# A hybrid block on one Trainium2 core: the second mixer's attention written as one pipeline of 16 heads, and a tile turned ahead of the output products

## The reference

```python
h = rmsnorm_2(x, mix_norm_g)
proj = h @ w_in
qa, ka, va, q_lat, kv_lat, k_r, g_a, g_b = jnp.split(proj, IN_OFFSETS, axis=-1)
qa, ka = apply_rope(qa), apply_rope(ka)               # 8 and 2 heads of 64
o_a = swa_sink_attention(qa, ka, va, sinks)           # 8 heads, window 128
qb = (rmsnorm_2(q_lat, q_norm_g) @ w_uq)              # 384 -> 8 heads of 96
kvb = (rmsnorm_2(kv_lat, kv_norm_g) @ w_ukv)          # 256 -> 8 x (64 key, 64 value)
o_b = mla_attention(q_nope, q_rope, k_nope, k_rope, vb)
y = sigmoid(g_a) * (o_a @ w_o_swa) + sigmoid(g_b) * (o_b @ w_o_mla)
x = x + y @ w_out
x = x + (silu(h @ w_gate) * (h @ w_up)) @ w_down      # h: x, normed again
```

## Time and profile before

| | us |
|---|---|
| median of 3 runs | 1191.82 (1191.3 to 1192.6) |
| the profiled execution | 1191.22 |
| its span in the trace | 1189.4 |
| TensorE matmuls busy | 1135.6 (95%) |
| TensorE weight loads busy | 952.0 (80%) |
| VectorE, ScalarE busy | 693.6 (58%), 587.9 (49%) |
| second mixer, from its norm to the last MLP's norm | 793.6 to 994 |

### The profile page before, as it was taken

How to read it: one execution, slowest core, us unless ns; L and a number is a source line. 1 busy time by engine, 2 the same in 40 slices (tenths; PEclk the granted TensorE clock), 3 DMA queues, 4 the chain that set the end, 5 groups by cost and what they waited for, 6 DMA issues and landing times. The chain is left out here.

```text
span 1189.4 us, 13875 instructions
## 1 busy us (share of the span) xinstructions
PE 1135.6 (95%) x5748; PEld 952.0 (80%) x5748; DVE 693.6 (58%) x777; ACT 587.9 (49%) x830; POOL 23.5 (2%) x35
## 2 busy tenths in 40 slices
PE   5999999999999999999899999999998889999997
PEld 4888887999989877777778888878887777888886
DVE  4644545676677777766575544466755266644443
ACT  4543335454577656654363444266565444444333
POOL 0000000000001100000000000000000000000000
PEclk9999999899999999999999999999998699999999
DMA  9666564555666553355456655545632235656650
GB/s 312 200 194 191 182 191 145 192 178 179 185 199 191 181 187 115 119 166 195 142 177 194 195 178 185 198 137 179 189 131 71 71 116 181 198 178 184 202 180 36
DMA packets 131150, 202.74 MB, mean 170 GB/s; under 512 B 5728, under 2 KB 98784, under 8 KB 130832
## 3 DMA queue, kind: packets, MB, share of 16 engines
q1 hardware_dynamic: 128272, 190.68, 49.9%
q0 software_dynamic: 2816, 11.18, 2.7%
HBM read 200.76 MB, written 1.08 MB: 170 GB/s over the span
## 5 line engine op out<-in xcount | busy, mean ns | idle before, releaser
L898 DVE TENSOR_TENSOR WL<-RAW,WH 128x2048 fp32r<-128x2048 f32 (+1 forms) x181 | 406.0, 2265 | 101.0 <-ACT WH L432 100.8
L432 ACT ACTIVATE WH<-RAW 128x2048 fp32r<-128x2048 f32 (+1 forms) x181 | 338.5, 1890 | 15.1 <-DMA RAW<-in_w_in 6.8
L1440 PE MATMUL PS<-WH,XTH 128*128 128x512 f32 (+1 forms) x700 | 277.7, 397 | 1.9 <-ACT V L622 1.9
L1442 PE MATMUL PS<-WH,XTL 128*128 128x512 f32 (+1 forms) x700 | 273.4, 391 | 0.0
L1441 PE MATMUL PS<-WL,XTH 128*128 128x512 f32 (+1 forms) x700 | 272.7, 390 | 0.0
L1440 PE MATMUL ACC<-WH,KTH 128*128 128x512 f32 (+1 forms) x466 | 186.9, 401 | 9.2 <-DVE KTL L987 6.0
L1441 PE MATMUL ACC<-WL,KTH 128*128 128x512 f32 (+1 forms) x466 | 184.0, 395 | 0.0
L1442 PE MATMUL ACC<-WH,KTL 128*128 128x512 f32 (+1 forms) x466 | 184.0, 395 | 0.0
L1440 PEld LDWEIGHTS PS<-WH,XTH 128*128 128x128 f32 x700 | 131.7, 188 | 28.2 <-ACT V L622 2.3
L1442 PEld LDWEIGHTS PS<-WH,XTL 128*128 128x128 f32 x700 | 131.5, 188 | 27.9
L1441 PEld LDWEIGHTS PS<-WL,XTH 128*128 128x128 f32 x700 | 131.8, 188 | 25.7
(11 more groups left out here) (258 smaller groups left out, 1287.3 us busy)
## 6 DMA issues: line engine op xcount, KB each, us to landing
RAW<-in_w_in SPq DMA_DIRECT2D x48, 1024.0 KB, 5.3
RAW<-in_ffn_w_gate SPq DMA_DIRECT2D x44, 512.0 KB, 4.0
RAW<-in_ffn_w_up SPq DMA_DIRECT2D x44, 512.0 KB, 5.0
RAW<-in_ffn_w_down SPq DMA_DIRECT2D x22, 1024.0 KB, 5.0
RAW<-in_w_gate SPq DMA_DIRECT2D x22, 512.0 KB, 4.1
RAW<-in_w_up SPq DMA_DIRECT2D x22, 512.0 KB, 5.1
RAW<-in_w_down SPq DMA_DIRECT2D x11, 1024.0 KB, 5.0
RAW<-in_ssd_w_branch SPq DMA_DIRECT2D x8, 1024.0 KB, 5.1
```

The source lines that it names most:

```text
L432: nc.scalar.activation(WH[:, s, 0:n], RAW[:, s, 0:n], ACT.Copy).then_inc(w_hi, 1)
L898: tt(WL[:, s, 0:n], RAW[:, s, 0:n], WH[:, s, 0:n].bitcast(F32), ALU.subtract).then_inc(w_lo, 1)
L1440: mm(ps, stat_hi, mov_hi, start=first, stop=False)
L1442: return mm(ps, stat_lo, mov_hi, start=False, stop=last)
```

## The change

**Second mixer, order of the units.** Input chunks are now 512, 512 and 416 columns wide: first the q latent with the window heads' keys, then their queries, then values, kv latent and rope key. The gate chunks `U_G2[0..3]` stand between the other units, the last one between `U_OSWA` and `U_OMLA`.

**Opening.** Each latent is squared, scaled and turned by itself (`latent_squares`, `latent_scale`, `latent_hi`, `latent_lo`); a table load for exp and tanh stands behind the second one. The first latent's squares go to V.

**16 heads in a row.** Round q of 18 does one head: `head_scores(q)` (bank 4), `turn_mla(q - 7)` in rounds 7 to 14, `cover(q)` (12 or 24 weight matmuls: gate pieces, `U_UKV`, `U_OSWA`), `head_values(q - 2)` (bank 6), `head_turn(q - 1)` (bank 5). Window heads are 0 to 7, latent heads 8 to 15. VectorE: `head_max(q)`, `head_sum(q - 1)`, `split_lo` in 11 of the rounds, mostly one after ScalarE's for the same unit, `head_out(q - 2)`. ScalarE: `head_exp(q)`, `split_hi`, gate copies, the copy of head q-1's turned probabilities. Three sets of small results (`head_sm`) and two score tiles take turns.

**Gates.** Copy and sigmoid become one tanh(x/2) as the chunk is copied; the product with a branch is (tanh + 1) times it, and the half is a scale of 0.5 where y is split for `U_OUT2`. y stays in BUF2. `branch_merge` runs in rounds 12 and 13.

**Both output products.** `by_pairs` has `then`: ahead of the last dozen branch matmuls TensorE waits for the first merged quarter and turns it; `second_merge` does product, sum, product, sum and then `kt_lo`; the list of `products` starts with that tile turned (`turned=True`), and its second extra split is at `j == 1`. In the second mixer `mla_piece(1, 1, first_out=True)` does this inside its 12 matmuls.

**First mixer's banks.** Value chunk 0 uses banks 0 and 1, gate chunk 0 banks 4 and 0, with earlier counts to wait for.

Core of the diff:

```diff
@@ banks
-            return ((4, 7), (4, 5), (6, 7), (4, 5))[n][t]
+            return ((4, 0), (4, 5), (6, 7), (4, 5))[n][t]
-            return ((5, 4), (7, 5))[n][t]
+            return ((0, 1), (7, 5))[n][t]
@@ TensorE, first mixer
-                    first_half(u, (v_bank(v, 0), v_bank(v, 1)), lambda t: pe.wait_ge(qkv_kept, ((7, 8), (8, 9))[v][t]))
+                    first_half(u, (v_bank(v, 0), v_bank(v, 1)), lambda t: pe.wait_ge(qkv_kept, 7) if v else pe.wait_ge(conv_done, 12))
-                        first_half(u, (4, 7), lambda t: pe.wait_ge(qkv_kept, 10 + t))
+                        first_half(u, (4, 0), lambda t: pe.wait_ge(qkv_kept, 8 + t))
@@ TensorE, by_pairs
                     if s < 3:
                         turn(s + 1)
+                    elif then:
+                        then()
                     pair_rows(u0 + s // 2 * 2, 1, s % 2, (n0 + s) % 2, False, s >= 2)
...
-            by_pairs(8, U_DAW, XN, turned=True)
-            by_pairs(12, U_WOUT, V, ready=lambda s: pe.wait_ge(merged, (1, 3, 2, 4)[s]))
+            def first_merged():
+                pe.wait_ge(merged, 1)
+                turn_tile(12, V, 0, 0)
+            by_pairs(8, U_DAW, XN, turned=True, then=first_merged)
+            by_pairs(12, U_WOUT, V, ready=lambda s: pe.wait_ge(merged, (1, 3, 2, 4)[s]), turned=True)
@@ VectorE, products and second_merge
-                        if j == n - 1:
+                        if j == 1:
                             split_lo()
...
-                product(0)
-                product(1)
-                own.wait()
-                add(0)
-                add(1)
+                for b in range(2):
+                    product(b)
+                    own.wait()
+                    add(b)
+                kt_lo(20 if m else 12, 0.5 if m else None)
@@ ScalarE, opening of the second mixer
+                if q == 5:
+                    act.wait_ge(proj_kept, 6)
+                    latent_squares(KL0, KV_RANK, 2)
+                    rsqrt(RS[:, 2:4], SS[:, 2:4], 2, lat_rs, 1.0)
+                    nc.scalar.preload_act_table_set("exp_and_others")
...
+            uq_keep(0)
+            split_hi()
             swa_keep(0)
+            uq_keep(1)
             swa_keep(1)
             swa_keep(2)
             split_hi()
+            act.wait_ge(lat_turned, 3)
+            act.wait_ge(w_used, U_UQ + 2)
+            latent_hi("kv_lat", [(7, 0), (7, 1)], (1,))
@@ VectorE, rounds
+            for q in range(18):
+                if q < 16:
+                    head_max(q)
+                if 1 <= q <= 16:
+                    head_sum(q - 1)
+                if q in (1, 2, 3, 5, 7, 9, 11, 12, 13, 15, 16):
+                    split_lo()
+                if q == 0:
+                    query_rope()
...
+                if q >= 2:
+                    head_out(q - 2)
@@ TensorE, before and in the rounds
+            pe.wait_ge(q_kept, 4)
+            g2_piece(0, 0, 0)
             pe.wait_ge(kdup_ok, 1)
+            turn_keys(6)
+            pe.wait_ge(lat_ok, 2)
             pe.wait_ge(swa_kept, 2)
+            turn_latent(7, KL0, 2)
+            pe.wait_ge(proj_kept, 6)
             pe.wait_ge(swa_kept, 3)
+            for q in range(18):
+                if q < 16:
+                    head_scores(q)
...
+                    turn_mla(q - 7)
+                if q < 17:
+                    cover(q)
+                if q >= 2:
+                    head_values(q - 2)
+                if 1 <= q <= 16:
+                    head_turn(q - 1)
```

More of the change, by code:

```diff
@@ L1243, in _ @@
             second_merge(0, BUF1, U_DAW + 3)
-            products(12, U_WOUT, 4)
+            products(12, U_WOUT, 4, turned=True)
             boundary(1, U_WOUT + 3, 4)
@@ L1284, in _, with latent_scale, latent_lo @@
-            dve.wait_ge(swa_roped, 1)
+            def latent_scale(c0, rank, ss, n):
+                dve.wait_ge(lat_rs, n)
+                for t in range(NT):
+                    a = PROJ[:, t, c0:c0 + rank]
+                    ins = ts(a, a, RS[:, ss + t:ss + t + 1], None, ALU.mult)
+                    own.inc(ins) if t == 0 else ins.then_inc(lat_ok, 1)
+            def latent_lo(name, banks, first, last):
+                for j, (bank, k) in enumerate(banks):
+                    dve.wait_ge(lat_hi, first if j < 2 else last)
+                    ins = stt(KTL[:, j * TOK:(j + 1) * TOK], PS[bank][:, k * TOK:(k + 1) * TOK],
+                              COLS[:, GC[name] + j:GC[name] + j + 1], KTH[:, j * TOK:(j + 1) * TOK].bitcast(F32),
+                              ALU.mult, ALU.subtract)
+                ins.then_inc(lat_lo, 1)
@@ new lines, in branch_merge, with head_max @@
+            def branch_merge(t):
+                dve.wait_ge(g2_kept, 4)
+                dve.wait_ge(w_used, U_OSWA + 2) if t else dve.wait_ge(tile_half, HALF[U_OSWA])
+                for h in range(2):
+                    a = BUF2[:, t, h * 512:(h + 1) * 512]
+                    stt(a, a, 1.0, PS[2 * t + h][:], ALU.add, ALU.mult).then_inc(acc_read, 1)
+            nsinks = ROWS[:, ROW["dt_bias"]:ROW["dt_bias"] + 8]
+            def head_max(q):
+                dve.wait_ge(sc2, q + 1)
+                if q >= 2:
+                    dve.wait_ge(p2_turned, q - 1)
+                mx, nmax, sums, sink, rec = head_sm(q)
+                r = q % SWA_HEADS
+                own.link(tt(SC[q % 2], PS[4][:, 0:384], tab("swa" if q < SWA_HEADS else "mla"), ALU.add))
+                for i in range(NT):
+                    own.inc(nc.vector.tensor_reduce(mx[:, i:i + 1], SC[q % 2][:, i * P:i * P + P * (i + 1)], AX.X, ALU.max))
+                own.wait()
+                if q < SWA_HEADS:
+                    ts(nmax, mx, -HD ** -0.5, nsinks[:, r:r + 1], ALU.mult, ALU.min).then_inc(s2_ready, 1)
+                else:
+                    ts(nmax, mx, -MLA_QK ** -0.5, None, ALU.mult).then_inc(s2_ready, 1)
@@ L1555, in pair_rows, with by_pairs @@
                     ins.then_inc(tile_half, 1)
-            def by_pairs(n0, u0, src, ready=None, turned=False):
+            def by_pairs(n0, u0, src, ready=None, turned=False, then=None):
                 def turn(s):
@@ L1773, in _ @@
[L1773 to L1780 removed]
+            pe.wait_ge(proj_kept, 4)
+            up_queries(1)
+            turn_queries(1, 7)
@@ L1855, in _ @@
+            cover(17)
+            pe.wait_ge(o2_kept, 16)
+            turn_rows(19, XN, 6)
+            mla_piece(0, 1)
+            pe.wait_ge(k_lo, 20)
+            mla_piece(1, 0)
+            mla_piece(1, 1, first_out=True)
+            by_pairs(20, U_OUT2, BUF2, ready=lambda s: pe.wait_ge(merged, 4 + (1, 3, 2, 4)[s]), turned=True)
             norm(4, U_FFN3)
```

615 lines of the change are left out of this document (320 added, 295 removed).

## The result

| | before | changed |
|---|---|---|
| median | 1191.56 us (4 runs) | 1169.09 us (1168.5 to 1170.6, 4 runs) |
| ratio | | 0.982, 95% interval 0.981 to 0.984 |
| the profiled execution | 1191.22 | 1170.61 |
| its span | 1189.4 | 1168.8 |

Faster by 22.5 us in the medians and by 20.6 in the two profiled executions. The forecast was 18.6 less, 1172.6, with a range of 1164 to 1184.

A forecast was written before the change was run, and what follows sets the result against it. TensorE, busy 95% of the span, was taken as the bound, with only its idle and low-clock time to win. Terms -1.6 - 2.8 - 2.1 - 7.7 - 3.1 - 1.3 = -18.6 gave 1172.6 us, range 1164 to 1184.

The forecast's parts named there:

- A: First mixer's gate chunk 0: the 1.92 us wait before it goes, between 0 and 1.9 won, taken as -1.6 us.
- B: First output product: its second weight unit starts earlier, though TensorE idles some 2 us for a split; -2.8 us.
- F: Second output product: same form as the first, TensorE idles 1.6 us, too short for the clock to fall; -3.1 us.
- C: Norm behind the first output product: an earlier split removes 1.7 of the 2.57 us gap and 0.4 of slow matmuls; -2.1 us.
- G: Norm behind the second mixer: the add moves 2.2 us forward and the 1.30 us gap closes; -1.3 us.
- E: Second mixer up to its branch's end: -11.1 us, less 3.4 for two dips of the clock, gives -7.7 us.
- E, the opening: Second mixer's start: TensorE waits 2.5 us for ScalarE's query copies and 3.2 before scores 1, each followed by low clock.
- E, the rounds: Second mixer's head rounds and what follows to the branch's end: 108.2 us, with covers narrowly hiding VectorE and ScalarE.
- q7 to q9 5.2 each: Second mixer's rounds 7 to 9: priced at 5.2 us each, 15.6 together.
- Rival 2: VectorE or ScalarE sets the second mixer's round: 0.85 us more in each of 16 rounds, 1186 us; chance 0.09.
- Rival 3: Clock stays at 1.2 GHz in the second mixer's chopped rounds, making the kernel slower: 1212 us; chance 0.04.
- rival 1: Smoother second-mixer opening: ScalarE's row overlaps better or the clock doesn't fall, 1166 us; chance 0.15.

The follow-up runs named there:

- Experiment 7: Changed kernel with the gate pieces of heads 13 and 14 moved to round 15, leaving two rounds without a cover: 1174.9 us.
- Experiment 5: Changed kernel with the second weight unit's low part computed earlier on VectorE in both output products: 1164.4 us.
- experiment 6: Changed kernel with the last split of both output products moved behind the norm's first residual sum: 1168.5 us.
- Experiment 2: Changed kernel with the doubled split of both output products back in their last step, as before: 1173.1 us.
- experiment 3: Changed kernel with ScalarE's table load moved from behind the kv latent's scale to just ahead of the copy of the turned keys: 1168.4 us.
- experiment 4: Changed kernel with two opening splits moved: ScalarE's behind the kv latent's high part, VectorE's behind head 0: 1164.9 us.
- experiment 8: Changed kernel with VectorE's mask sum of every head done three times, 1.1 us more a round for 16 rounds: 1174.9 us.

## Why the prediction was right, and where not

- **What bounds the kernel** held: TensorE's own work stayed, and its idle time and low clock went. Experiment 7 shows it from the other side. No run takes the rest of the second mixer's change apart (one head a round, the order of the units, the tanh in place of the sigmoid), so how its 13.1 us divide among them is not shown.
- **A, B and F** held, their new gaps too: a split was forecast to make TensorE idle some 2 us in the middle of the first product and 1.6 in the second, and it did, 1.88 and 1.57. Experiment 5 took both away, but for 0.22 in the second. A and B together gave 4.9 for 4.4. A turn by TensorE that stands behind gate chunk 0 and ahead of the product tells the two apart (442.10 before, 440.37 now, with the first mixer's start 0.5 later): A gave 2.2 for the 1.6 forecast, 0.3 above its upper bound of 1.9, and B 2.7 for 2.8. Where the 0.3 comes from is not shown. F's gap was called too short for the clock by the rows. No low clock came behind it, but one came behind the gap of the same 1.57 us before the norm, so the length alone was no ground for it.
- **C was too high**: 1.1 instead of 2.1, and a low clock of 1.7 on top. The step that failed is "It could begin 2.25 sooner, but ScalarE's squares of the same tile finish only about 1.7 before". The 1.7 was right. What was missed is that the one split left would no longer start right behind the turned tile's low part: it now waits for its own high part from ScalarE,

```profile
589.78 0.69 DVE L1002 TENSOR_TENSOR KTL<-PS,KTH 128x512 fp32r<-128x512 f32 x1 [1.78 <-ACT KTH L530]
591.59 2.29 DVE L913 TENSOR_TENSOR WL<-RAW,WH 128x2048 fp32r<-128x2048 f32 x1 [1.11 <-ACT WH L437]
593.80 1.22 DVE L959 TENSOR_TENSOR SCR<-ACC,GAIN 128x1024 f32<-128x1024 f32 x1
```

  where before, in the earlier trace rows, it followed at once, because VectorE was a unit behind. The gain product begins 0.6 later than the squares would let it, as experiment 6 shows. Experiment 2 measures the term: 1.0 us of idle. The 0.4 of slow matmuls, the other part of C, did not show.
- **G** was forecast to close the gap of 1.30; 0.47 of it stayed, the same waiting split: with the split elsewhere, in experiment 6, that gap was gone.
- **E, the opening**, held almost to the tenth. Waits of 2.5 and 3.2 us were forecast, 1.94 and 3.08 came, and both causes are shown by experiments 3 and 4. The forecast for head 0's scores, counted from the norm, was 48.4 us (and 1.7 for a low clock); measured 48.0. The one thing that did not come is that low clock, behind the 1.94 us gap. By the 2.66 us for a switch on the Trainium skill's page "ScalarE: Activation LUTs", section "What ACT_TABLE_LOAD costs", the estimate for this gap was 3.9; experiment 3 shows the switch at its row's 1.28.
- **E, the rounds.** Window heads were forecast at 4.76 and took 4.74 to 4.76. The term that was mis-sized is "q7 to q9 5.2 each", and with it those of q10 to q14. Round 7, whose scores are still a window head's, took 5.03; rounds 8 and 9 took 4.81 instead of 5.2, 10 and 11 8.02 instead of 8.4, 12 7.53 instead of 8.0. All small pieces had been priced by those of the window heads and by rows where each waits for a semaphore. A latent head's round:

```profile
915.71 0.39 PE L1852 MATMUL PS<-QK 96*128 96x128 f32 x2
915.93 0.60 PE L1853 MATMUL PS<-QK 96*128 96x256 f32 x2
916.37 0.60 PE L1885 MATMUL PS<-TAB,SCR 128*96 128x128 f32 x4
919.58 0.33 PE L1875 MATMUL PS<-V,GAIN 128*128 128x64 f32 x2
...
920.19 0.50 PE L1861 MATMUL PS<-TAB,BUF 128*128 128x128 f32 x3
920.52 0.39 PE L1852 MATMUL PS<-QK 96*128 96x128 f32 x2
```

  Scores 0.66 (forecast 0.85), values 0.61 (0.77), the turn 0.33 (0.36). That is 0.39 a round, 3.0 us in rounds 2 to 14, and 3.2 to the branch's end. With the 1.7 of the clock, 0.4 of the opening and 0.2 for the gap before head 1 and the dip behind it, both a little smaller than forecast, that is 5.5, for the 5.4 between -7.7 and -13.1.
- **The rivals.** Rival 2 (VectorE or ScalarE sets the round) is refuted: VectorE was forecast busy 4.3 us in a split round and is 3.7 to 4.1 where it does not merge (4.6 and 5.1 in rounds 11 and 12, which last 8.0 and 7.5), and even 1.1 us more a round costs nothing there (experiment 8). It decides somewhere between 1.1 and 2.2. Rival 3 (the clock stays down in chopped rounds) is refuted by the windows: 1.00 in all of them. Of rival 1 half came true, one of two low clocks.

The errors of C (too hopeful by 2.7) and E (too careful by 5.4) had opposite signs. The total of the sum is therefore better than its parts, and that is luck.

## What to carry to other kernels

Where a list on VectorE or ScalarE is written by hand, price each split with its own input: a split moved out of a late engine's queue finds its high part not ready, and the gain is the smaller of the two. When a change removes a long wait, look for the work that stands ahead of the next wanted result only by order; here such places (splits ahead of a wanted copy or maximum, a table load, a split behind two products) were worth 11.4 of 1169 us together and took a moved line each. And a chain of small steps hid behind 12 matmuls a round at full clock here, while two rounds made bare lost 3.9 us: 0.3 in one, and 3.6 in the other, where VectorE had a split and a merge in front of the result that TensorE wanted.
